# Where the 128-column blocks of the expert weights stand: two at the end of each unit, or eight in every fourth unit

## The reference, cut to what matters

```python
def moe_swiglu(h, router_w, w_gate, w_up, w_down):
    xt = h.reshape(B * T, D)
    top_val, top_idx = lax.top_k((xt @ router_w).astype(jnp.float32), TOP_K)
    combine = ...                      # softmax of the two, spread over the experts
    for e in range(N_EXPERTS):
        y = y + combine[:, e:e + 1] * swiglu(xt, w_gate[e], w_up[e], w_down[e])
```

## Time and profile before

| | us |
|---|---|
| median of 3 runs | 1575.26 (1574.97 to 1576.73) |
| the profiled execution | 1578.41 |
| its span, first to last instruction | 1576.6 |
| mean granted clock of TensorE | 0.997 |
| TensorE busy with matmuls | 1511.0 |
| TensorE's weight loads | 1306.0 |
| VectorE, ScalarE, GpSimd busy | 253.9, 177.2, 143.3 |
| read from memory | 428.89 MB |

### The profile page before, as it was taken

The page is one execution under the profiler, slowest core; times in us unless marked ns, Lnnn a source line. Parts: engine busy times, 40 slices in busy tenths (PEclk is TensorE's granted clock), DMA queues, the critical chain, the costliest instruction groups (busy, mean ns, idle before and its releaser), DMA issues.

```text
span 1576.6 us, 51984 instructions
## 1 busy us (share of the span) xinstructions
PE 1511.0 (96%) x24693; PEld 1306.0 (83%) x24693; DVE 253.9 (16%) x490; ACT 177.2 (11%) x383; POOL 143.3 (9%) x167
## 2 busy tenths in 40 slices
PE   9999999999999999999999999999999999999987
PEld 7786587777687864989999899999999999898886
DVE  3433310000143434100000100100100100100102
ACT  4123120000131332200000000000000000000001
POOL 2243200000022522200000000000000000000000
PEclk9999999999999999999999999999999999999999
DMA  9213344444243144999999999999999999999993
GB/s 342 90 49 134 107 161 160 160 160 148 80 174 107 55 158 188 358 387 388 373 367 373 365 362 384 357 363 371 370 377 379 365 380 368 364 373 379 384 391 142
DMA packets 133602, 433.31 MB, mean 275 GB/s; under 512 B 9082, under 2 KB 33916, under 8 KB 119052
## 3 DMA queue, kind: packets, MB, share of 16 engines
q1 hardware_dynamic: 132384, 427.69, 72.6%
q0 software_dynamic: 672, 2.14, 0.5%
q10 hardware_dynamic: 332, 0.13, 0.0%
HBM read 428.89 MB, written 1.05 MB: 273 GB/s over the span
## 4 chain that ended last, share of the span: by engine, by line
PE 93%; issue 3%; DVE 2%; ACT 1%; POOL 1%; DMA 0%; ACTq 0%; DVEq 0%
PE ps L1144 35%; PE ps L1179 18%; PE ps L1000 9%; PE ps L699 8%; PE ps L1011 4%; PE ps L862 4%; PE ps L710 3%; PE ps L1221 2%; PE ps L819 1%; PE ps L1080 1%; PE ps L732 1%; PE ps L829 1%; PE ps L695 1%; PE ps L725 1%; PE ps L839 1%
## 5 line engine op out<-in xcount | busy, mean ns | idle before, releaser
L1144 PE MATMUL ps<-wpost,ring 128*64 128x80 f32 (+1 forms) x5040 | 215.0, 237 | 8.6 <-issue 7.1
L1144 PE MATMUL ps<-AT_sb,ring 128*64 128x80 f32 x5104 | 211.9, 236 | 11.5 <-issue 11.4
L1144 PEld LDWEIGHTS ps<-AT_sb,ring 128*64 128x64 f32 x5104 | 205.1, 141 | 20.4 <-issue 17.6
L1144 PEld LDWEIGHTS ps<-wpost,ring 128*64 128x64 f32 (+1 forms) x5040 | 208.1, 142 | 16.5 <-issue 11.5
L1179 PEld LDWEIGHTS ps<-LT_sb,ring 128*64 128x64 f32 (+1 forms) x5104 | 203.9, 140 | 19.1 <-issue 15.4
L1179 PE MATMUL ps<-LT_sb,ring 128*64 128x80 f32 (+1 forms) x5104 | 210.9, 236 | 8.7 <-issue 7.9
L1000 PEld LDWEIGHTS ps<-hT_sb,ring 128*128 128x128 f32 x768 | 136.0, 190 | 24.6 <-issue 9.1
L1000 PE MATMUL ps<-hT_sb,ring 128*128 128x256 f32 (+1 forms) x768 | 155.7, 362 | 0.0
L699 PE MATMUL ps<-hT_sb,ring 128*128 128x256 f32 x576 | 128.2, 380 | 0.0
L699 PEld LDWEIGHTS ps<-hT_sb,ring 128*128 128x128 f32 x576 | 108.1, 190 | 15.0 <-DVE late L1657 0.5
L2008 POOL TENSOR_SCALAR small<-small 128x1 f32<-128x1 f32 x16 | 3.8, 240 | 1189.6 <-ACT late L1535 918.8
(11 more groups left out here) (285 smaller groups left out, 1097.7 us busy)
## 6 DMA issues: line engine op xcount, KB each, us to landing
ring<-in_moe_w_gate SPq DMA_DIRECT2D x84, 1024.0 KB, 8.4
ring<-in_moe_w_up SPq DMA_DIRECT2D x84, 1024.0 KB, 8.7
ring<-in_moe_w_down SPq DMA_DIRECT2D x84, 1024.0 KB, 8.5
late<-in_moe_w_up SPq DMA_DIRECT2D x28, 1024.0 KB, 8.1
late<-in_moe_w_gate SPq DMA_DIRECT2D x28, 1024.0 KB, 9.1
late<-in_moe_w_down SPq DMA_DIRECT2D x28, 1024.0 KB, 8.4
ring<-in_ffn_w_gate SPq DMA_DIRECT2D x11, 1024.0 KB, 5.4
ring<-in_ffn_w_up SPq DMA_DIRECT2D x11, 1024.0 KB, 8.1
```

The source lines that it names most:

```text
L1144: return mm(o[lo:lo + width, :], pairs[:, m % 2, lo:lo + width], xgT[e % 2][:, k, :], start=(k == 0 and m % 4 == 0), stop=(k == KD - 1), s ...
```

## The change

Every unit below `LAST_WIDE` gets two wide blocks, as the last two of its sixteen, and the blocks keep one order, first index k (or i), second index m. `unit_calls`, `first_call`, `pe_order` and `page_turns` follow from `wide_blocks`, so the marks and the turns are worked out anew. The wait for the gathered inputs stays ahead of the first block of k = 0 and of k = 4.

```diff
+import itertools
...
+WIDE_BLOCKS = 2
...
 def wide_blocks(n):
-    return UNIT_BLOCKS // 2 if n % 4 == 3 and n < LAST_WIDE else 0
+    return WIDE_BLOCKS if n < LAST_WIDE else 0
...  in m_in
-                    wide = wide_blocks(n) // len(ks)
-                    for k in ks:
-                        if kind == "g" and c == 0 and k % 4 == 0:
+                    narrow = UNIT_BLOCKS - wide_blocks(n)
+                    for i, (k, m) in enumerate(itertools.product(ks, range(MOE_TILES[c]))):
+                        if kind == "g" and c == 0 and k % 4 == 0 and m == 0:
                             pe.wait_ge(xg_ready, per_round(r, 2 * e + k // 4 + 1, 2 * N_EXP))
-                        for m in range(wide, MOE_TILES[c]):
-                            for lo in (0, P // 2):
-                                ins = block(k, m, lo, P // 2)
-                                turned(ins, e, f"{kind}{c}", call)
-                                call += 1
-                    for k in ks:
-                        for m in range(wide):
-                            ins = block(k, m, 0, P)
+                        for lo in (0, P // 2) if i < narrow else (0,):
+                            ins = block(k, m, lo, P // 2 if i < narrow else P)
                             turned(ins, e, f"{kind}{c}", call)
                             call += 1
                     ins.then_inc(unit_used, 1)
...  in m_down
-                    wide = wide_blocks(n) // 2
-                    for i in range(2):
-                        for m in range(wide, KD):
-                            for lo in (0, P // 2):
-                                ins = block(i, m, lo, P // 2)
-                                turned(ins, e, f"d{c}", call)
-                                call += 1
-                    for i in range(2):
-                        for m in range(wide):
-                            ins = block(i, m, 0, P)
+                    narrow = UNIT_BLOCKS - wide_blocks(n)
+                    for at, (i, m) in enumerate(itertools.product(range(2), range(KD))):
+                        for lo in (0, P // 2) if at < narrow else (0,):
+                            ins = block(i, m, lo, P // 2 if at < narrow else P)
                             turned(ins, e, f"d{c}", call)
                             call += 1
                     ins.then_inc(unit_used, 1)
```

## The result

The changed kernel takes 1601.45 us (median of 4 runs, 1600.5 to 1606.61) against 1575.12 us beside it (1573.18 to 1576.73): a ratio of 1.0178 with a 95% interval of 1.0158 to 1.0199. That is slower by some 26 to 28 us, where +39.7 was forecast (1615).

What follows compares the result with a forecast made beforehand. The prediction took TensorE's own stepping plus stalls on late instructions in the expert stage as the bound. Wide blocks and edges at +66.7 us less 27 us of stalls gave +39.7 us, so 1615 us, range 1594 to 1640.

Steps and rivals of the forecast that it cites:

- What bounds the kernel: Expert stage: TensorE's own stepping plus stalls on late instructions, 33 us, set the end; no weight transfer is waited for.
- Number of blocks, order, releases: Expert stage: 584 wide blocks become 588, no wait is added, and freeing each buffer some 0.5 us later costs nothing.
- The price of a block and of an edge: TensorE, expert stage: 0.092 us a wide block, 0.30 us a cluster for entering and leaving; +66.7 us together.
- The bound of 0.42: Expert stage: upper bound in us of a cluster's edge cost, if short clusters never reach the steady step; +102 us.
- B: Expert stage: short clusters pay only half to three quarters of the edge cost; 1575 to 1595 us, chance 0.11.
- C: First wide record of each unit: edges vanish, fetches and loads set the pace; -22 us, 1553, chance 0.05.
- What the even spread gives back: Expert stage: pages all last 5.77 us, so most of 33 us of stalls go, 6 us stay; -27 us.
- 47 us for all else: TensorE's time in experts 0 to 6 besides narrow units, wide blocks with edges, and stalls; the same after the change.
- A: Expert stage: half or more of the 33 us of stalls remain; +50 to +67, 1625 to 1642 us, chance 0.14.
- D: Expert stage: transport sets the pace before and after, about 2.75 us a unit; no difference, chance 0.05.
- The sum: Whole kernel: +66.7 us of TensorE work less 27 us of stalls is +39.7 us, giving 1615 us.
- The signs named beforehand: Experts 1 to 6 about 120 us each, "issue" under 8, units 2.65 to 2.75, packets every 5.9, last expert 121 to 122.

Runs made afterwards that it cites:

- the runs without contention: From the 17th unit on, weight transfers of 4 KB instead of 1 MB, in the kernel before (1519.14 us) and in the changed kernel (1587.23 us).

## Why the prediction had the mechanism right and the size half too large

The time lies inside the stated range, 1594 to 1640 us, and the way it moved was forecast; the forecast difference was 13 us too large.

*What bounds the kernel.* Right. No wait of TensorE for a landing appears in the expert stage of any profile here, and the stalls are late instruction pages: they went with the transfers, at the same instructions.

*Number of blocks, order, releases.* Right, and worth nothing that can be measured, as said: the order alone gives 0.9997.

*The price of a block and of an edge.* Right. +66.7 us were summed up from single records of the profile before; the runs without contention give +65.2. The edge of 0.30 us, carried over from clusters of 16 records to clusters of 4, is (830.0 - 764.8) / 219 = 0.298 us from 16 records to 4 and 0.305 from 4 to 2. The bound of 0.42 and rivals B and C are excluded. A block is about 0.09 us, where 0.092 was taken.

*What the even spread gives back.* Here the prediction failed, in size: -27 us were counted, and 804.2 - 764.8 - 0.7 = 38.7 us came back. There are two halves. First, I left 6 us of stalls for fetches late for other reasons, which no row showed, and 0.7 us were left: with 5.77 us in every page there is one wait of 0.2 us in the list. Second, I summed the stalls before as 33 us, from the list of waits plus 0.17 us each, and they were 39.4. The missing 6.4 us went into my "47 us for all else"; the run without transfers has 764.8 - 648.2 - 75.6 = 41.0 us for it.

Where the 6.4 us are can be counted. The kernel before and the same kernel with small transfers issue the same matmuls, so the starts of their records can be laid side by side, one by one but for a few that a trace lacks, and each place where the first falls behind the second is a delay. The 35 waits of the list are worth 35.7 us so, 0.24 us each above their idle time and not 0.17. Thirteen more delays of 0.1 to 0.4 us, 3.1 us together, are not in the list: a record lasts 0.233 us by its modelled end, and a short delay hides beneath it. The rest of the stage has 0.5 us. So both the price of a listed stall and the number of stalls were too low.

*The rivals.* A, that stalls stay, is the opposite of what happened. D, that transport sets the same pace before and after, is wrong for this pair: the kernel before lost 39 us to the transfers, the changed one 0.7. It comes near for the kernels with less work on TensorE. Without wide blocks a unit took 813.1 / 292 = 2.78 us, and at the 377 GB/s of that stage a unit needs 2.78 us; but TensorE waited on "issue" there, not for a landing, and no run tells the pace of transport from that of late fetches.

*The sum.* +65.2 - 38.7 = +26.5 us in the stage and +0.8 in the last expert, +27.3 in all. In the profiles 3.7 us of it are hidden by an earlier start of the stage; that start lies anywhere between 632.8 and 637.6 us in the profiles of twelve kernels that are the same up to there, so it is scatter. The medians differ by 26.3 us.

*The signs named beforehand* came true: experts 1 to 6 at about 120 us (the chain of expert 3 runs from 984.2 to 1104.1 us), "issue" below 8 us, 2.69 and 2.72 us a unit, a packet per 5.89 us, 121.5 us for the last expert. Six experts at 120 us are only 23 us more than the 697 us from 744.5 to 1441.2 us that they took before. I never held that against +39.7; it would have shown that the sum and the sign did not agree.

## What to carry to other kernels

Work that is put in only to give something else time pays twice: by its amount, and by the number of times the engine has to change over to it. Spreading it evenly removed nearly every stall here and still lost, as 219 more changeovers cost 65 us and the stalls to be won were 39. Before such a spread, price one changeover from single records, multiply, and hold it against the whole of what can be won. Take the latter as the difference to a run in which the contention is removed, not as the sum of the listed waits, which leaves out the short ones and prices the others too low. Of the spreads tried, the best had one cluster of three or four blocks in every two units, so about one in each page: half the clusters of the changed kernel, and no run of narrow pages as with 16 in every eighth unit. It beat the kernel before by 0.3%.

## What the runs showed of the hardware

A change between 64-column and 128-column stationary matrices in float32 with 80 moving columns costs 0.30 us in and out, whether 2, 4 or 16 records stand between. By these prices, as an estimate, a single 128-column block between narrow ones takes 0.139 + 0.09 + 0.30 = 0.53 us, longer than three blocks in halves (0.42 us).

TensorE's instructions come in packets of 16 KB. While weight transfers keep the DMA engines at 0.99, pages that last 4.45 us stall it two times in three (100 waits in 151 pages), for 0.94 us of idle time each; with pages of 5.8 us there was one wait of 0.2 us in 141; and with 7 GB/s of transfers there was none, with pages of 4.45 us among them.

A long stall can cost more than itself: after waits of 2.4 and 1.6 us the granted clock stood at 1.2 GHz for 10.3 and 6.8 us.
